# A gated attention mixer's silu, written as z/(1+exp(-z)): the exponential on ScalarE, the rest on VectorE

## The chip, the core and the metric
The kernel runs on one core of a Trainium2 chip. The core has five engines that run side by side: TensorE (PE, matmuls; PEld is its weight load), VectorE (DVE), ScalarE (ACT), GpSimd (POOL) and SyncE (SP), which here issues the DMAs. They are held in order by semaphores only. The metric is the device time of one execution in microseconds (us), lower is better.

## The reference
Two blocks of two layers each, on 256 tokens of width 1024, in float32. The first block (attention, short convolution, state-space scan, feed-forward) is not touched. The second block has two mixers; the first (`mixer_a`, three dilated window attentions) is not touched either. The change is in `mixer_b`, the second mixer: a sliding-window attention with 16 heads and 2 key heads, whose output is multiplied by the silu of a gate z and then projected.

```python
def mixer_b(x, w_in, sinks, w_out, cos, sin):
    q, k, v, z = split_cols(x @ w_in, [B_WIDTH, B_KV, B_KV, B_WIDTH])
    q = apply_rope(q.reshape(B_, S, B_HEADS, HEAD_DIM), cos, sin).reshape(B_, S, B_KV_HEADS, G, HEAD_DIM)
    k = apply_rope(k.reshape(B_, S, B_KV_HEADS, HEAD_DIM), cos, sin)
    v = v.reshape(B_, S, B_KV_HEADS, HEAD_DIM)
    o, _ = banded_attention(q, k, v, B_WINDOW - 1, sinks)
    o = o.reshape(B_, S, B_WIDTH).astype(x.dtype)
    return (o * jax.nn.silu(z)) @ w_out
```
silu(z) is z/(1+exp(-z)). After the mixer come a layer norm, a gated projection of a second input, and the output.

## The kernel before
The host code makes one list `steps`, and every engine walks through this one list in its order and emits its own part of each step. So the order on each engine is fixed by hand. A matrix product is cut into *units* of 256 output columns. The weights of a unit are loaded by SyncE into one of three `raw` buffers and split in two halves (k 0 to 3 and 4 to 7), each into a rounded part `whi` (ScalarE copy, L1592) and a rest `wlo` (VectorE subtraction, L2157). TensorE then does three matmuls for each product (`mm3`, L1050 to L1052: hi x hi, hi x lo, lo x hi), 24 of 256 columns for each half of a unit, into one of the PSUM banks 0 to 2 in turn. Bank 5 takes the attention output, banks 3, 4, 6 and 7 the scores and transposes.

In the second mixer (`i == 1`, L812 to L821) the units are, in this order: keys and values `bkv`, queries aq0, aq1, aq2, gate az0, query aq3, gates az1, az2, az3, and then the output projection `out2` with four units. Each gate unit is two blocks of 128 gate channels by 256 tokens, in one bank (128x512 in float32). The attention goes by *pairs* of heads, p = 0 to 7, whose steps are set between the halves of the units by `b_slots` (L783):
- `att2_first`, `att2_second`: scores on TensorE (L1416); on VectorE mask and maximum (L2731), sinks and sign (L2742, L2744, L2748); on ScalarE the exponential with its sum (L2011) and that of the sink (L2016).
- `att2_turn`: VectorE adds the sink and takes the reciprocal of the sums, four numbers for each of 128 partitions (L2760, L2761); GpSimd multiplies the probabilities by it (L2926); TensorE transposes them (L1444) into banks 4 and 7; ScalarE copies them out to `APT` (L2035).
- `att2_pv`: TensorE multiplies by the values into bank 5 (L1470, L1473); VectorE multiplies this by the gate's silu `AZ` into `YA` (L2781); ScalarE rounds it to `HA` (L2041), VectorE takes the rest `LA` later (L2179). `out2` reads HA and LA.

A pair's pv may not start before VectorE has read the one before out of bank 5 (`acquire(5, (s_ya, ip))`, L1455). The gate unit az`hq` serves pairs 2hq and 2hq + 1: az0 is needed first by pair 0, az1 by pair 2, az2 by pair 4, az3 by pair 6. ScalarE takes the silu of a gate unit from its bank to `AZ[hq % 2]` as soon as its turn in the list comes (L1746 to L1749), and signals `s_z2`; both the bank and the product at L2781 are released by that signal. VectorE has nothing to do for a gate unit but the weight splits that stand ahead of every unit (`unit`, L2223), and the deferred pieces in `late`. `chain` (L2168) on VectorE makes the next instruction wait for the one just issued.

In the slots around the gate units, in this order: az0, then pv of pair 0 and the scores of pair 4; half of aq3, pv of pair 1; ...; az1, pv 2, scores of pair 7; half of az2, pv 3; az2, pv 4; half of az3, pv 5; az3, pv 6; first half of the first out2 unit, pv 7.

Of the kernel before, what the change touches and what calls it, by code (L numbers as in the profile page):

```python
# [17 lines left out]
ALU = mybir.AluOpType  # L18
# [151 lines left out]
def build(nc, A, out, counts):  # L170
# [151 lines left out]
    s_ya = signal("ya")  # L322
    s_yh = signal("yh")
    s_z2 = signal("z2")


    base = (nc.sbuf_base + 63) // 64 * 64
# [576 lines left out]
    def both(b):  # L904

        return b.rearrange("p (b t) -> p b t", b=2)
# [669 lines left out]
    def _(engine):  # L1576
# [52 lines left out]
        def unit(u):  # L1629
# [67 lines left out]
            elif kind == "ff1":  # L1697
                l, g, i = u.key
                t = t_of(l)
                sl = slice(t[0], t[1])  # L1700
                for bi in (0, 1):
                    j = 2 * i + bi
                    b = bank(u, bi)
                    if j >= 2:
                        act.wait_ge(s_fq, s_fq.at((l, g, j - 2)))
                    elif g > 0:
                        act.wait_ge(s_fq, s_fq.at((l, g - 1, 6 + j)))
                    f(R32[j % 2][:, sl], b[:, 0:t[1] - t[0]], ACT.Relu).then_inc(*s_relu.tick(u.key + (bi,)))
                for bi in (0, 1):
                    j = 2 * i + bi  # L1710
                    act.wait_ge(s_relu, s_relu.at(u.key + (bi,)))
                    f(hi_part("f", l, None, j, sl), R32[j % 2][:, sl], ACT.Square).then_inc(*s_fh.tick((l, g, j)))
            elif kind == "ff2":
                l, g, i = u.key
                if g == 3:
                    for m in (2 * i, 2 * i + 1):
                        late.append(lambda l=l, m=m: square_y(l, "ffn", m))
                    for m in (2 * i, 2 * i + 1) if i < 3 else ():
                        late.append(lambda l=l, m=m: gate_y(l, "ffn", m))
            elif kind in ("aq", "ak") or kind == "bkv":  # L1720
                n = 2 if kind != "bkv" else 1
                b = both(bank(u, n - 1))
                key = u.key + ((kind,) if kind != "bkv" else ("kb",))
                if sh_turn[0] >= 2:
                    act.wait_ge(s_rope2, s_rope2.at(("n", sh_turn[0] - 2)))
                for q in range(4):
                    o = q ^ 1
                    ins = f(SH[sh_turn[0] % 2][32 * q:32 * q + 32, 0:n, :], b[32 * o:32 * o + 32, 0:n, :], ACT.Copy)  # L1728
                ins.then_inc(*s_sh2.tick(key))
                sh_turn[0] += 1  # L1730
                if kind == "bkv":
                    for tt in (0, 1):
                        b = bank(u, 1)
                        b = banks[bank_of[(u.id, 1 + tt)]]

                        src = b[:, 0:P].rearrange("p (h d) -> p h d", h=2)
                        for dup in (0, 1):
                            ins = f(AV[0][:, 0:2, tt, 64 * dup:64 * dup + 64], src, ACT.Copy)
                        ins.then_inc(*s_vb2.tick(tt))
            elif kind == "av":  # L1740
                i, hq, g = u.key
                if hq >= 2:
                    act.wait_ge(s_o2, s_o2.at((i, 2 * (hq - 2) + 1)))
                f(AV[hq % 2][:, g, :, :], both(bank(u, 1)), ACT.Copy).then_inc(*s_v2.tick(u.key + (0,), u.key + (1,)))
            elif kind == "az":
                i, hq, g = u.key  # L1746
                if hq >= 2:
                    act.wait_ge(s_ya, s_ya.at((i, 2 * (hq - 2) + 1)))
                f(AZ[hq % 2], both(bank(u, 1)), ACT.Silu).then_inc(*s_z2.tick(u.key + (0,), u.key + (1,)))  # L1749
            elif kind == "proj":  # L1750
                i, part = u.key
                for n in range(2):
                    if n == 1:
                        splits(u.halves_next)
                    m = 2 * part + n
                    f(PJ[:, 2 * m:2 * m + 2, :], both(bank(u, n)), ACT.Copy).then_inc(*s_pj.tick((i, m)))
                splits(u.halves_ahead)
            elif kind == "gate":
                i, j = u.key
                if j >= 2:  # L1760
                    act.wait_ge(s_gmul, s_gmul.at((i, j - 2)))
                f(SH[j % 2], both(bank(u, 1)), ACT.Sigmoid).then_inc(*s_sg.tick(u.key))
                if i == 0:
                    def part():
                        act.wait_ge(s_x2_new, s_x2_new.at((0, 2 * j + 1)))
                        f(parts2("x2", 1)[0][:, 2 * j:2 * j + 2, :], XT[:, 2 * j:2 * j + 2, SEQ:T], ACT.Copy)\
                            .then_inc(*s_x2_hi.tick((1, 2 * j), (1, 2 * j + 1)))

                    late.append(part)
# [374 lines left out]
    def _(engine):  # L2144
# [78 lines left out]
        def unit(u):  # L2223
# [70 lines left out]
            elif kind == "ff2":  # L2294
                l, g, i = u.key
                t = t_of(l)
                sl = slice(t[0], t[1])
                for bi in (0, 1):
                    m = 2 * i + bi
                    if u.packed:  # L2300
                        y, b, keys = YM[:, 2 * i:2 * i + 2, sl], both(bank(u, 1)), (u.key + (0,), u.key + (1,))
                    else:
                        y, b, keys = YM[:, m, sl], bank(u, bi)[:, 0:t[1] - t[0]], (u.key + (bi,),)
                    if bi == 0 or not u.packed:
                        if g == 0:
                            ins = v.tensor_copy(y, b)
                        else:
                            dve.wait_ge(s_f_add, s_f_add.at((l, g - 1, i, bi)))
                            ins = v.tensor_tensor(y, y, b, ALU.add)
                        ins.then_inc(*s_f_add.tick(*keys))  # L2310
                    if g == 3 and m < KC - 2:
                        late.append(lambda m=m: add_square(("p", l, "ffn"), m, sl))
            elif kind in ("aq", "ak", "bkv"):
                if kind != "aq" or u.key[0] == 0:
                    rope_unit(u)
            elif kind == "out2":
                i, j = u.key
                v.scalar_tensor_tensor(out=V32[:, 2 * j:2 * j + 2, :], in0=XT[:, 2 * j:2 * j + 2, SEQ:T], scalar=ALPHA, in1=both(bank(u, 1)),
                                       op0=ALU.mult, op1=ALU.add).then_inc(*s_v32.tick(u.key + (0,), u.key + (1,)))
                for bi in (0, 1):  # L2320
                    m = 2 * j + bi

                    def add(i=i, m=m):
                        dve.wait_ge(s_v32, s_v32.at((i, m // 2, m % 2)))
                        total = RR[0][:, 0, :]
                        if m == 0:
                            ins = v.tensor_copy(total, V32[:, 0, :])
                        else:
                            dve.wait_ge(s_ln_acc, s_ln_acc.at((i, "mean", m - 1)))
                            ins = v.tensor_tensor(total, total, V32[:, m, :], ALU.add)  # L2330
                        ins.then_inc(*s_ln_acc.tick((i, "mean", m), *([(i, "mean")] if m == KC - 1 else [])))

                    late.append(add)
            elif kind == "proj":
                splits(u.halves_ahead)
            elif kind == "gate":
                i, j = u.key
                m = slice(2 * j, 2 * j + 2)
                dve.wait_ge(s_sg, s_sg.at(u.key))
                dve.wait_ge(s_pj, s_pj.at((i, j)))  # L2340
                dve.wait_ge(s_ln_x, s_ln_x.at((i, 2 * j + 1)))
                v.tensor_tensor(RR[j % 2], SH[j % 2], PJ[:, m, :], ALU.mult).then_inc(*s_gmul.tick((i, j)))
                dve.wait_ge(s_gmul, s_gmul.at((i, j)))
                v.tensor_tensor(XT[:, m, SEQ:T], XT[:, m, SEQ:T], RR[j % 2], ALU.add).then_inc(*s_x2_new.tick((i, 2 * j), (i, 2 * j + 1)))
                if i == 0:
                    def part():
                        dve.wait_ge(s_x2_hi, s_x2_hi.at((1, 2 * j + 1)))
                        dve.wait_ge(s_x2_new, s_x2_new.at((0, 2 * j + 1)))
                        hi, lo = parts2("x2", 1)
                        rest(lo[:, m, :], XT[:, m, SEQ:T], hi[:, m, :], s_parts2.tick((1, 2 * j), (1, 2 * j + 1)))  # L2350

                    late.append(part)
# [619 lines left out]
```

## Time and profile before
| | |
|---|---|
| median of 3 runs | 1640.62 us (1637.44 to 1644.46) |
| profiled execution, its own time | 1640.4 us |
| its span | 1638.4 us |
| TensorE busy | 1518.7 us (93%) |
| VectorE busy | 971.9 us (59%) |
| ScalarE busy | 914.6 us (56%) |
| GpSimd busy | 34.2 us (2%) |
| mean granted TensorE clock | 0.969 |

The profile is one execution; all times in the rows are microseconds from the start of its span unless they are marked ns. The second mixer's work lies from about 1476 us (its first queries and keys) to about 1569 us (where TensorE goes on with its output projection). A granted clock of 1.00 is 2.4 GHz, 0.50 is 1.2 GHz. ACT_TABLE_LOAD on ScalarE loads the tables of another set of functions.

### The profile page before, as it was taken

The numbers are of one execution on the slowest core, as the hardware profiler recorded it, in microseconds if no ns is written. First come the engines' busy times: TensorE is split into PE (matmuls) and PEld (weight loads), VectorE is DVE, ScalarE is ACT, GpSimd is POOL, SyncE is SP. The second block draws the span as 40 slices with busy tenths as digits, with TensorE's granted clock in tenths as the row PEclk, the third lists the DMA queues.
The fourth block names the chain that finished last, engine by engine and source line by source line (L and its number), as shares of the span: only waits on it lengthen the run. The fifth ranks groups of instructions, "written<-read, shape, count | busy, mean of one in ns | idle before, by whom it ended". The sixth has DMA issues, their size and how long they took to land.

```text
span 1638.4 us, 25449 instructions
## 1 busy us (share of the span) xinstructions
PE 1518.7 (93%) x10131; PEld 1273.4 (78%) x10131; DVE 971.9 (59%) x1565; ACT 914.6 (56%) x1510; POOL 34.2 (2%) x74
## 2 busy tenths in 40 slices
PE   5999998989999999979988899998999999889887
PEld 3687455758888888838855799998999999888787
DVE  2464567473343434474767766667676767577555
ACT  5654666462232423464665655566786868377745
POOL 3000000000000000000000000000000000001200
PEclk9999899989999999999998999998999999999999
DMA  7731445342433233343316576653634434343332
GB/s 248 236 102 52 155 151 184 121 136 79 153 103 100 81 103 103 111 129 88 118 38 198 181 228 189 197 196 120 232 130 155 155 131 153 104 155 106 101 103 78
DMA packets 223638, 225.37 MB, mean 138 GB/s; under 512 B 8234, under 2 KB 222064, under 8 KB 223472
## 3 DMA queue, kind: packets, MB, share of 16 engines
q1 hardware_dynamic: 222816, 223.63, 42.3%
q8 instruction: 80, 1.31, 0.3%
q14 instruction: 38, 0.31, 0.1%
q0 software_dynamic: 704, 0.12, 0.0%
HBM read 222.68 MB, written 1.05 MB: 137 GB/s over the span
## 4 chain that ended last, share of the span: by engine, by line
PE 72%; DVE 13%; ACT 10%; issue 2%; DMA 1%; POOL 1%; DVEq 0%; ACTq 0%; POOLq 0%
PE bank L1050 21%; PE bank L1052 20%; PE bank L1051 20%; DVE wlo L2157 2%; PE bank L1098 2%; ACT whi L1592 2%; ACT SH L1728 1%; PE bank L1256 1%; PE bank L1416 1%; PE bank L1444 1%; PE bank L1371 1%; ACT AP L2011 1%; POOL vrow L2904 1%; DVE AP L2731 1%; DMA raw<-in_w_out_dram 1%
## 5 line engine op out<-in xcount | busy, mean ns | idle before, releaser
L2157 DVE TENSOR_TENSOR wlo<-raw,whi 128x1024 fp32r<-128x1024 f32 (+2 forms) x322 | 387.9, 1208 | 258.5 <-ACT whi L1592 253.5
L1592 ACT ACTIVATE whi<-raw 128x1024 fp32r<-128x1024 f32 (+2 forms) x322 | 336.0, 1046 | 272.8 <-PE bank L1052 250.0
L1050 PE MATMUL bank<-HH,whi 128*128 128x512 f32 (+2 forms) x640 | 245.9, 384 | 19.9 <-DVE HL L2179 16.9
L1051 PE MATMUL bank<-HL,whi 128*128 128x512 f32 (+2 forms) x640 | 242.2, 378 | 0.0
L1052 PE MATMUL bank<-HH,wlo 128*128 128x512 f32 (+2 forms) x640 | 241.8, 378 | 0.0
L1050 PE MATMUL bank<-HA,whi 128*128 128x256 f32 x576 | 165.2, 287 | 13.8 <-DVE LA L2179 5.2
L1051 PE MATMUL bank<-LA,whi 128*128 128x256 f32 x576 | 162.1, 281 | 0.0
L1052 PE MATMUL bank<-HA,wlo 128*128 128x256 f32 x576 | 161.9, 281 | 0.0
L1050 PEld LDWEIGHTS bank<-HH,whi 128*128 128x128 f32 (+1 forms) x640 | 121.1, 189 | 49.3 <-issue 17.8
L1052 PEld LDWEIGHTS bank<-HH,wlo 128*128 128x128 f32 (+1 forms) x640 | 121.3, 190 | 23.6 <-issue 0.5
L1051 PEld LDWEIGHTS bank<-HL,whi 128*128 128x128 f32 (+1 forms) x640 | 121.3, 190 | 22.5 <-issue 0.9
L1050 PEld LDWEIGHTS bank<-HA,whi 128*128 128x128 f32 x576 | 111.0, 193 | 17.8 <-issue 11.6
L1051 PEld LDWEIGHTS bank<-LA,whi 128*128 128x128 f32 x576 | 111.1, 193 | 0.0
L1052 PEld LDWEIGHTS bank<-HA,wlo 128*128 128x128 f32 x576 | 110.9, 192 | 0.0
L1050 PE MATMUL bank<-FH,whi 128*128 128x512 f32 x256 | 100.3, 392 | 0.0
L1051 PE MATMUL bank<-FL,whi 128*128 128x512 f32 x256 | 99.7, 389 | 0.0
L1052 PE MATMUL bank<-FH,wlo 128*128 128x512 f32 x256 | 99.6, 389 | 0.0
L1050 PE MATMUL bank<-HX,whi 128*128 128x256 f32 x320 | 90.8, 284 | 4.3 <-DVE HXL L2179 4.3
L1051 PE MATMUL bank<-HXL,whi 128*128 128x256 f32 x320 | 89.9, 281 | 0.0
L1052 PE MATMUL bank<-HX,wlo 128*128 128x256 f32 x320 | 89.9, 281 | 0.0
L1050 PE MATMUL bank<-YH,whi 128*128 128x256 f32 x264 | 78.0, 296 | 5.1 <-DVE YL L2883 4.5
L1728 ACT ACTIVATE SH<-bank 32x512 f32<-32x512 f32 (+1 forms) x116 | 67.5, 582 | 16.9 <-PE bank L1052 15.4
(377 smaller groups left out, 3077.2 us busy)
## 6 DMA issues: line engine op xcount, KB each, us to landing
raw<-in_w_ff_dram SPq DMA_DIRECT2D x64, 1024.0 KB, 5.4
raw<-in_w_mod_dram SPq DMA_DIRECT2D x48, 1024.0 KB, 5.2
raw<-in_a_w_in_dram SPq DMA_DIRECT2D x40, 1024.0 KB, 5.1
raw<-in_w_in_dram SPq DMA_DIRECT2D x18, 1024.0 KB, 5.3
raw<-in_b_w_in_dram SPq DMA_DIRECT2D x9, 1024.0 KB, 5.3
raw<-in_w_out_dram SPq DMA_DIRECT2D x8, 1024.0 KB, 5.4
raw<-in_ple_w_gate_dram SPq DMA_DIRECT2D x8, 1024.0 KB, 5.3
raw<-in_a_w_out_dram SPq DMA_DIRECT2D x4, 1024.0 KB, 5.1
```

What stands on the lines that cost most here:

```text
L1050: nc.tensor.matmul(o, wh, xh, start=start, stop=False, skip_group_check=shared)
L1051: nc.tensor.matmul(o, wh, xl, start=False, stop=False, skip_group_check=shared)
L1052: return nc.tensor.matmul(o, wl, xh, start=False, stop=stop, skip_group_check=shared)
L1098: ins = nc.tensor.matmul(b[32 * q:32 * q + 32, 0:256], cs[:, k, :], raw[u.id % RAW_SLOTS][:, k * 256:k * 256 + 256], start=turn == 0, stop ...
L1256: nc.tensor.matmul(b[:, 0:nk], QT[0:QK, h, q0:q0 + P], KT[0:QK, h, 0:nk], start=True, stop=True)\
L1371: nc.tensor.matmul(b[:, 0:t[1] - t[0]], ones, SQ[k % 2][:, t[0]:t[1]], start=k == 0, stop=k == KC - 1)\
L1416: ins = nc.tensor.matmul(dst[e][:, g * n:(g + 1) * n], q_, k_[:, 0:n], start=True, stop=True)
L1444: ins = nc.tensor.transpose(b[:, to:to + P], att_p(ip, e)[:, src:src + P], ident)
L1592: f(whi[h % HALF_SLOTS][:, 0:n], raw[u.id % RAW_SLOTS][:, (h % 2) * n:(h % 2) * n + n], ACT.Copy)\
L1728: ins = f(SH[sh_turn[0] % 2][32 * q:32 * q + 32, 0:n, :], b[32 * o:32 * o + 32, 0:n, :], ACT.Copy)
L2011: f(p_[:, a:a + n], p_[:, a:a + n], ACT.Exp, bias=small[:, neg:neg + 1], scale=SCALE, accum_out=small[:, total:total + 1]).then_inc(*s_e2. ...
L2157: v.tensor_tensor(wlo[h % HALF_SLOTS][:, 0:n], raw[u.id % RAW_SLOTS][:, (h % 2) * n:(h % 2) * n + n], whi[h % HALF_SLOTS][:, 0:n].bitcast( ...
```

## The change
For the units az0 to az3 of the second mixer ScalarE writes exp(-z) instead of silu(z) to `AZ`, and signals a new semaphore `s_ez2`. VectorE, when the unit's turn comes in its own list (behind the unit's splits and the deferred pieces), adds 1, takes the reciprocal, and multiplies by z read from the bank, all in place in `AZ`, each instruction waiting for the one before. The last of them gives the signal `s_z2` that ScalarE gave before; so the bank is held until then too. The first mixer keeps its silu. Nothing else is moved.

```diff
@@ -322,6 +322,7 @@
+    s_ez2 = signal("ez2")
@@ -1746,7 +1747,10 @@
                 i, hq, g = u.key
                 if hq >= 2:
                     act.wait_ge(s_ya, s_ya.at((i, 2 * (hq - 2) + 1)))
-                f(AZ[hq % 2], both(bank(u, 1)), ACT.Silu).then_inc(*s_z2.tick(u.key + (0,), u.key + (1,)))
+                if i == 0:
+                    f(AZ[hq % 2], both(bank(u, 1)), ACT.Silu).then_inc(*s_z2.tick(u.key + (0,), u.key + (1,)))
+                else:
+                    f(AZ[hq % 2], both(bank(u, 1)), ACT.Exp, scale=-1.0).then_inc(*s_ez2.tick(u.key))
@@ -2313,6 +2317,12 @@
             elif kind in ("aq", "ak", "bkv"):
                 if kind != "aq" or u.key[0] == 0:
                     rope_unit(u)
+            elif kind == "az" and u.key[0] == 1:
+                z = AZ[u.key[1] % 2]
+                dve.wait_ge(s_ez2, s_ez2.at(u.key))
+                chain(v.tensor_scalar(z, z, 1.0, None, ALU.add))
+                chain(v.reciprocal(z, z))
+                v.tensor_tensor(z, both(bank(u, 1)), z, ALU.mult).then_inc(*s_z2.tick(u.key + (0,), u.key + (1,)))
             elif kind == "out2":
```

## Rows read from the trace of the kernel before
**Rows 1.** The page, part 4: shares of the chain that ended last.
```profile
PE 72%; DVE 13%; ACT 10%; issue 2%; DMA 1%; POOL 1%; DVEq 0%; ACTq 0%; POOLq 0%
```
**Rows 2.** Windows: length, busy PE, PEld, DVE, ACT, POOL; clock; DMA share, GB/s.
```profile
1520.00:1530.00 10.00, 7.03 (x50) 6.86 (x50) 5.24 (x18) 8.12 (x25) 1.90 (x4) 0.83 0.02 4
```
**Rows 3.** Groups by line, ScalarE: its table loads; count, busy us, mean ns, idle before.
```profile
L1749 ACT ACT_TABLE_LOAD x7 | 9.0, 1283 | 1.7 <-PE bank L1052 1.7
L2011 ACT ACT_TABLE_LOAD x7 | 9.0, 1283 | 9.2 <-DVE small L2744 6.5 <-DVE small L2736 2.6
```
**Rows 4.** Timeline of ScalarE, second mixer: start us, length us, what, idle before.
```profile
1514.39 1.28 ACT L1749 ACT_TABLE_LOAD   x1
...
1518.87 1.28 ACT L2011 ACT_TABLE_LOAD   x1 [1.52 <-DVE small L2744]
...
1539.71 1.28 ACT L1749 ACT_TABLE_LOAD   x1 [0.27 <-PE bank L1052]
1541.01 0.60 ACT L1749 ACTIVATE AZ<-bank 128x512 f32<-128x512 f32 x1
...
1545.23 1.28 ACT L2011 ACT_TABLE_LOAD   x1 [1.66 <-DVE small L2744]
...
1551.14 1.28 ACT L1749 ACT_TABLE_LOAD   x1
...
1558.66 0.60 ACT L1749 ACTIVATE AZ<-bank 128x512 f32<-128x512 f32 x1 [0.26 <-PE bank L1052]
```
**Rows 5.** Timeline of VectorE, second mixer, around the four gate units.
```profile
1515.00 0.18 DVE L2761 RECIPROCAL small<-small 128x4 f32<-128x4 f32 x1
1516.41 0.42 DVE L2781 TENSOR_TENSOR YA<-bank,AZ 128x256 f32<-128x256 f32 x1 [1.23 <-ACT AZ L1749]
...
1540.08 0.18 DVE L2761 RECIPROCAL small<-small 128x4 f32<-128x4 f32 x1
1541.74 0.42 DVE L2781 TENSOR_TENSOR YA<-bank,AZ 128x256 f32<-128x256 f32 x1 [1.48 <-ACT AZ L1749]
...
1552.63 0.43 DVE L2179 TENSOR_TENSOR LA<-YA,HA 128x256 fp32r<-128x256 f32 x1
1553.17 0.42 DVE L2781 TENSOR_TENSOR YA<-bank,AZ 128x256 f32<-128x256 f32 x1
...
1558.06 2.36 DVE L2157 TENSOR_TENSOR wlo<-raw,whi 128x1024 fp32r<-128x1024 f32 x2
1560.45 0.42 DVE L2781 TENSOR_TENSOR YA<-bank,AZ 128x256 f32<-128x256 f32 x1
```
**Rows 6.** Timeline of TensorE: pv of pairs 1, 5, 7, transposes of pair 3, restart.
```profile
1516.89 0.65 PE L1470 MATMUL bank<-APT,AV 128*64 128x256 f32 x4 [0.90 <-DVE YA L2781]
...
1525.42 1.51 PE L1444 MATMUL bank<-ident_sb,AB 128*128 128x128 f32 x6 [2.97 <-ACT APT L2035]
...
1553.65 0.65 PE L1470 MATMUL bank<-APT,AV 128*64 128x256 f32 x4 [0.45 <-DVE YA L2781]
...
1562.32 0.65 PE L1470 MATMUL bank<-APT,AV 128*64 128x256 f32 x4
...
1568.90 0.43 PE L1050 MATMUL bank<-HA,whi 128*128 128x256 f32 x1 [2.76 <-DVE wlo L2157]
```
**Rows 7.** Groups of VectorE by form: count, busy us, mean ns, idle before.
```profile
L2205 DVE TENSOR_TENSOR RR<-bank,rope_sb 128x512 f32<-128x512 f32 x28 | 19.4, 691 | 30.7 <-ACT SH L1728 27.0 <-PE bank L1052 3.5
...
L2358 DVE TENSOR_SCALAR CV<-XP,VT 128x512 f32<-128x512 f32 x12 | 5.8, 486 | 7.7 <-ACT XP L1672 7.5
...
L2761 DVE RECIPROCAL small<-small 128x4 f32<-128x4 f32 x8 | 1.4, 178 | 0.3
...
L2557 DVE RECIPROCAL RD<-DN 128x64 f32<-128x64 f32 x2 | 1.1, 552 | 0.1
```
**Rows 8.** Timeline of GpSimd: its products for pair 7.
```profile
1552.74 2.07 POOL L2926 TENSOR_TENSOR AP<-AP,small 128x128 f32<-128x128 f32 x4 [10.44 <-DVE small L2761]
```
**Rows 9.** Line L2742 alone: ns min/median/max of its 16 instructions.
```profile
L2742 DVE TENSOR_SCALAR small<-small,sinks_sb x16: 215/225/682, 1491.6 to 1544.7; 128x2 f32<-128x2 f32 x16
```

## The prediction
> **What bounds the kernel now.** I read four things. First the page's chain of the work that ended last: TensorE holds 72% of it, VectorE 13%, ScalarE 10% [rows 1]. This share is an average over a kernel of some 1,640 us, and the change touches only the second mixer, so the next question is what the chain looks like there. The chain listed in order of time goes, between 1484 and 1569 us, mostly through ScalarE and VectorE: a score's maximum on VectorE, an exponential on ScalarE, a silu, a product on VectorE, a weight split. The windows say the same in numbers: TensorE is busy for 7.03 of the 10 us from 1520 [rows 2], where its transposes waited 2.97 us for ScalarE's copy APT [rows 6]. There TensorE waits for the other two; a microsecond put on VectorE between them is felt.
>
> Then the two engines' timelines. ScalarE runs 7 table loads before silus (L1749) and 7 before attention exponentials (L2011) in the whole kernel [rows 3]. Of these, the second mixer has the five listed at 1514.39, 1518.87, 1539.71, 1545.23 and 1551.14 [rows 4], and one more before its first exponential, which stays. On VectorE one sees who stands behind the silu: the products YA<-bank,AZ at 1516.41, 1541.74, 1553.17 and 1560.45 (pairs 0, 2, 4 and 6, the first users of each gate unit) [rows 5]. The first two start 0.12 to 0.13 us after the silu's end (1541.01 + 0.60 = 1541.61, product at 1541.74) [rows 4, 5]. And behind the product stands TensorE: bank 5 holds the attention output of one pair, and the next pair's pv matmul may not start before the product has read it. pv of pair 1 had waited 0.90 us for the product, pv of pair 5 0.45 us [rows 6].
>
> **What is removed.** Four silus become four exponentials of the same shape; I count them at the same 0.60 us [rows 4]. Exp is already the function at L2011 and Copy ran after it without a load, so behind that first load no switch is left in the mixer: five loads go, 5 x 1.283 = 6.4 us of ScalarE. From start of load to start of silu is 1541.01 - 1539.71 = 1.30 us, and I use 1.3 for each that lies on the path. The Trainium skill, page "ScalarE: Activation LUTs", section "What ACT_TABLE_LOAD costs", adds a drain of about 1380 ns to every switch, 2.66 us together. By it each of the path's loads would give back 1.36 us more. The rows show no such drain: the load at 1539.71 is followed by the silu 0.02 us after its end. What the rule would give is a rival below.
>
> **What is added.** Per gate unit, on VectorE, one after the other: an addition, a reciprocal and a product, each on 128x512 numbers, each waiting for the one before.
> - The addition: TENSOR_SCALAR 128x512 takes 486 ns [rows 7].
> - The product with one operand in PSUM: TENSOR_TENSOR 128x512 RR<-bank takes 691 ns [rows 7].
> - The reciprocal of 128x512: the trace has none. The largest is 128x64 with 552 ns, the next 128x4 with 178 ns [rows 7]. The slope is (552 - 178) / 60 = 6.23 ns for each number of a partition, so 178 + 508 x 6.23 = 3.34 us. Taken in proportion it would be 8 x 552 = 4.42 us. The lower end is the rate of the other operations, some 0.69 us. I take 3.34, because the 128x64 row is already far above the cost of an ordinary operation and a fixed start-up plus a slope fits both rows.
> The page "VectorE: DVE Perf Modes" of the Trainium skill, section "First, the fixed hardware budget", says that the reciprocal is an iterative divide with a repeat count of 8. With 8 times the (0.69 - 0.42) / 256 = 1.05 ns that a product takes per number [rows 5, 7] that is, as an estimate, 8.4 ns and 4.5 us, and the sum would be that of the first rival; the rows here say about 6 times, not 8, and I stay with the rows. It is the rule that speaks most against this change.
> With two gaps of 0.03 us (L2760 to L2761 is such a pair) the added piece is 0.49 + 3.34 + 0.69 + 0.06 = 4.58 us, 18.3 us of VectorE in all, for 6.4 us of ScalarE. The two are not on the path alike, so I walk the path, with "+" for the delay against the trace of before.
>
> **Unit 0.** Exp may start at 1514.39 and ends at 1514.99, but VectorE is free only after its reciprocal of pair 3 (1515.00 + 0.18) [rows 5]. So 1515.21 + 4.58 = 1519.79, and the product of pair 0 starts at 1519.82 instead of 1516.41: +3.4. Queued behind it on VectorE: pair 4's maximum, then pair 1's product. TensorE's pv of pair 1 goes from 1516.89 to 1520.3. Pair 4's exponential loses its table load: 3.4 - 1.3 = +2.1, and ScalarE's splits, copies and the exponentials of pairs 5 and 6 follow it in order, all +2.1. TensorE's own lateness is absorbed: its next transposes (1525.42) waited 2.97 us for ScalarE [rows 6] and get only ScalarE's +2.1.
>
> **Unit 1.** Exp starts at 1539.71 + 2.1 = 1541.81 without a load, ends at 1542.41; VectorE is free at 1540.08 + 0.18 + 2.1 = 1542.36, so it is just the Exp that counts. Plus 0.13, 4.58 and 0.03: pair 2's product at 1547.15 instead of 1541.74, +5.4. Pair 7's maximum stands behind it, and pair 7's exponential loses its load: 5.4 - 1.3 = +4.1.
>
> **Unit 2.** ScalarE's Exp is early (its load gone as well), so this saving is worth nothing: VectorE arrives at the unit only with the end of LA at 1552.63 + 0.43 + 4.1 = 1557.16. Here GpSimd works in parallel on pair 7, from 1552.74 + 4.1 = 1556.84 for 2.07 us [rows 8]. A TENSOR_SCALAR beside GpSimd's products was held up: L2742 took 682 ns at most beside them, 215 at least [rows 9]. So the addition gets 0.46 us more. 1557.19 + 0.46 + 4.58 = 1562.23, product of pair 4 at 1562.26 instead of 1553.17: +9.1. TensorE's pv of pair 5, before at 1553.65, stands idle in front of it for about 6 us.
>
> **Unit 3.** Its Exp waits for TensorE to end the unit: 1558.66 + 9.1 = 1567.8 at full clock. After the idle piece before 1525.42 the clock was at half speed for about a third of a 10 us window (granted clock 0.83 from 1520 to 1530 [rows 2], that is 1.2 instead of 2.4 GHz for 3.4 us, 1.7 us lost), and this stall is longer; so +1.7, Exp from 1569.5 to 1570.1. VectorE's splits end at 1558.06 + 2.36 + 9.1 = 1569.5. The piece runs from 1570.2 to 1574.8, product of pair 6 at 1574.8 instead of 1560.45: +14.3. Without the half clock it would be VectorE that counts, and +13.7.
>
> **The end.** pv of pair 7 started at 1562.32 although its bank was free at 1560.45 + 0.42 = 1560.87: 1.45 us of slack, 1.3 after a signal's 0.13. So 14.3 - 1.3 = +13.0 for it. From there to TensorE's restart at 1568.90 [rows 6] all is a chain: product of pair 7, its copy, two splits. Nothing behind 1569 knows the change, so +13.0 carries to the end. The profiled execution's own time is 1640.4 us (span 1638.4), and the median of the runs is 1640.62, the same. 1640.4 + 13.0 = 1653.4.
>
> **The rivals.**
> - The reciprocal costs 4.42 us instead of 3.34. For it: the proportion with the 128x64 row. Against: the 128x4 row shows a small fixed part only. Four units in series: 4 x 1.08 = +4.3, so 1657.7.
> - The large reciprocal runs as fast as other operations, 0.69 us (not slower). For it: no row of a large one exists. Against: 128x64 took 552 ns. The place is the four pieces; each is then 1.93 us. The same walk gives +0.8, -0.5, +0.1, -1.2, +1.2, +3.1 and at the end +1.8: 1642.2. It decides from about 2.2 us of reciprocal downward, since every microsecond of it counts some four times and +8.2 is the bound below.
> - A switch holds ScalarE longer than its load. The most that a row allows is the idle 1.52 us ahead of the load at 1518.87 [rows 4], if that were a drain and not, as listed, a wait for the maximum. On the path lie three switches (pairs 4 and 7, unit 1): 3 x 1.5 = 4.5 more given back, +8.5; with some of unit 0's, about 1648. Against it: the maximum really ends just there, and nothing lies between load and silu. This is the page's drain as named above; its figure would give nearly the same.
> - The change doesn't do what it says: Exp at L1749 and Exp at L2011 would still be separated by loads. Then 3 x 1.3 + 1.1 come back: 1658.4. Against: it is the same function.
> - GpSimd holds the addition for its whole stretch, in units 1 and 2: 1.9 + 1.3 = +3.2, so 1656.6. I keep it within the forecast's range.
>
> **How the numbers follow.** The forecast 0.69, the dearer reciprocal 0.13, not separated by function 0.03; these are slower. The cheap reciprocal 0.12 and the longer switch 0.02 lie within 0.5%. 0.5% is 8.2 us, about what a measurement of this kernel can tell from no change (the runs of before spread by 7 us). Faster by that would need more than all five loads give (6.4 us), so 0.01. Slower 0.85, same 0.14, faster 0.01. Range: low 1648, for a reciprocal near 2.2 us; without half clock and GpSimd's lock it would be 1652.4. High 1660: the dearer reciprocal and most of GpSimd's term.
>
> **What would show it.** ScalarE: table loads at the gate line only 4 instead of 7, at L2011 5 instead of 7. VectorE: four reciprocals 128x512, 3.3 us each, starting right behind the addition. TensorE: a wait of some 6 us for the product before pv of pair 5, of 4 us before that of pair 1, and a half clock behind the first of them. The second mixer (from 1476 to the restart near 1569) is 13 us longer and nothing before or after differs. I am wrong if the reciprocal is off by a factor, since the sum is nearly four times its length, or if TensorE's waits for YA products do not grow.

## The result and the profile after
The changed kernel takes 1656.7 us (median of 7 runs, 1648.35 to 1659.81); the kernel before takes 1643.33 us in the same 7 rounds (1637.44 to 1645.64). The ratio is 1.0083 with a 95% interval of 1.0066 to 1.0100, so by the ratio the change costs 13.6 us, between 11 and 16 (the medians differ by 13.4). The forecast was +13.0 us and 1653.4 us. It started from 1640.4 us, and the kernel before has since measured 1643.33 us, so 2.9 of the 3.3 us between 1653.4 and 1656.7 are the starting point's.

The page of the changed kernel, parts 1 and 4. The first lines are busy us, share of the span and count of each engine; the last is the chain that ended last.

```profile
span 1657.5 us, 25464 instructions
## 1 busy us (share of the span) xinstructions
PE 1529.9 (92%) x10131; PEld 1284.8 (78%) x10131; DVE 989.6 (60%) x1577; ACT 908.1 (55%) x1505; POOL 34.7 (2%) x74
...
PE 71%; DVE 15%; ACT 10%; issue 2%; DMA 1%; POOL 1%; DVEq 0%; ACTq 0%; POOLq 0%
```
VectorE is busy 989.6 - 971.9 = 17.7 us longer, ScalarE 914.6 - 908.1 = 6.5 us shorter, and VectorE has two points more of the chain [rows 1]. But nothing here says that the one falls on the path and the other only in part. For that the groups and the timelines are needed. The groups by line that answer to [rows 3] and the new ones of [rows 7] (count, busy us, mean ns, idle before):

```profile
L2015 ACT ACT_TABLE_LOAD x5 | 6.4, 1283 | 6.0 <-DVE small L2754 3.3 <-DVE small L2746 2.6
L1751 ACT ACT_TABLE_LOAD x4 | 5.1, 1283 | 1.6 <-PE bank L1053 1.6
...
L2324 DVE RECIPROCAL AZ<-AZ 128x512 f32<-128x512 f32 x4 | 13.4, 3353 | 0.1
L2325 DVE TENSOR_TENSOR AZ<-bank,AZ 128x512 f32<-128x512 f32 x4 | 2.8, 692 | 0.1
L2323 DVE TENSOR_SCALAR AZ<-AZ 128x512 f32<-128x512 f32 x4 | 1.8, 446 | 0.8 <-ACT AZ L1753 0.7
```
Table loads before exponentials 5 instead of 7, before the gates 4 (all in the first mixer) instead of 7, as forecast. The reciprocal takes 3353 ns, where 3.34 us were worked out from its 128x64 and 128x4 rows.

VectorE around units 0 and 2, the timeline that answers to [rows 5]:

```profile
1519.87 0.18 DVE L2771 RECIPROCAL small<-small 128x4 f32<-128x4 f32 x1
1520.08 0.43 DVE L2323 TENSOR_SCALAR AZ<-AZ 128x512 f32<-128x512 f32 x1
1520.55 3.35 DVE L2324 RECIPROCAL AZ<-AZ 128x512 f32<-128x512 f32 x1
1523.93 0.69 DVE L2325 TENSOR_TENSOR AZ<-bank,AZ 128x512 f32<-128x512 f32 x1
1524.66 0.42 DVE L2791 TENSOR_TENSOR YA<-bank,AZ 128x256 f32<-128x256 f32 x1
...
1552.24 0.42 DVE L2791 TENSOR_TENSOR YA<-bank,AZ 128x256 f32<-128x256 f32 x1
...
1562.31 0.51 DVE L2323 TENSOR_SCALAR AZ<-AZ 128x512 f32<-128x512 f32 x1
1562.85 3.35 DVE L2324 RECIPROCAL AZ<-AZ 128x512 f32<-128x512 f32 x1
1566.24 0.69 DVE L2325 TENSOR_TENSOR AZ<-bank,AZ 128x512 f32<-128x512 f32 x1
1566.96 0.42 DVE L2791 TENSOR_TENSOR YA<-bank,AZ 128x256 f32<-128x256 f32 x1
...
1579.45 0.42 DVE L2791 TENSOR_TENSOR YA<-bank,AZ 128x256 f32<-128x256 f32 x1
```
And TensorE, which answers to [rows 6]: the first scores, pv of pairs 1, 3, 5 and 7, the transposes of pair 3 and the restart.

```profile
1493.98 0.93 PE L1417 MATMUL bank<-AK,AQ 64*128 64x128 f32 x8 [2.04 <-DVE AQ L2217]
...
1525.13 1.12 PE L1471 MATMUL bank<-APT,AV 128*64 128x256 f32 x4 [4.27 <-DVE YA L2791]
...
1533.31 0.82 PE L1445 MATMUL bank<-ident_sb,AB 128*128 128x128 f32 x6
...
1552.72 0.65 PE L1471 MATMUL bank<-APT,AV 128*64 128x256 f32 x4 [0.71 <-DVE YA L2791]
...
1567.44 1.12 PE L1471 MATMUL bank<-APT,AV 128*64 128x256 f32 x4 [6.48 <-DVE YA L2791]
...
1579.93 0.65 PE L1471 MATMUL bank<-APT,AV 128*64 128x256 f32 x4 [2.11 <-DVE YA L2791]
...
1586.50 0.58 PE L1051 MATMUL bank<-HA,whi 128*128 128x256 f32 x1 [2.68 <-DVE wlo L2161]
```
Before pv of pairs 1 and 5, where TensorE had waited 0.90 and 0.45 us for the product [rows 6], it now waits 4.27 and 6.48 us; before pv of pairs 3 and 7, where it had not waited, 0.71 and 2.11 us. The four matmuls behind the two long waits take 1.12 instead of 0.65 us: the clock has fallen. The wait of the transposes for ScalarE (2.97 us [rows 6]) is gone in return. The windows show TensorE's short busy time and the granted clock of 0.72 and 0.77 (columns as in [rows 2]):

```profile
1520.00:1530.00 10.00, 5.73 (x31) 3.84 (x30) 8.12 (x21) 3.22 (x11) 2.22 (x5) 0.72 0.30 100
1560.00:1570.00 10.00, 3.52 (x22) 2.61 (x21) 8.00 (x11) 3.40 (x7) 2.25 (x4) 0.77 0.33 105
```

The two profiled spans differ by 1657.5 - 1638.4 = 19.1 us, more than the medians. To see what belongs to the change I measure a **stretch**: from the first scores of the second mixer on TensorE to the restart behind pair 7. Before, the scores start at 1489.12 (the same row of the kernel before is shown with the repeat below) and the restart is at 1568.90 [rows 6], 79.78 us. After, 1586.50 - 1493.98 = 92.52 us. So 12.7 us lie in the stretch, 4.9 us ahead of it, where no line was changed, and 1.5 us behind it. The experiments are read by this stretch. It is steadier than a whole run, but not exact: a second profile of the kernel before gives 81.0 instead of 79.8 us, one of the changed kernel 92.5 again (last experiment). So the change costs 11.5 to 12.7 us in the stretch, and a difference of about 1 us between two profiles can be the execution's.

Most of that uncertainty has one place: the piece from the scores of pair 6 to pv of pair 2 on TensorE, the same 32 matmuls in every kernel. It took 5.34 us in the first profile of before, at a granted clock of 0.68, and 6.57 us in the second, at 0.54; time times clock is 3.6 and 3.5, so the clock accounts for the difference. It is called **the clock's place** below.

### The profile page after: what moved, and what is told of

It is laid out like the page before. It is cut to its first block, busy times and chain, and to the rows that moved or that the text cites. A ratio compares the mean times of both kernels' runs of the same rounds, so it can differ in the third digit from the quotient of the medians.

```text
span 1657.5 us, 25464 instructions
## 1 busy us (share of the span) xinstructions
PE 1529.9 (92%) x10131; PEld 1284.8 (78%) x10131; DVE 989.6 (60%) x1577; ACT 908.1 (55%) x1505; POOL 34.7 (2%) x74
## 3 DMA queue, kind: packets, MB, share of 16 engines
q8 instruction: 80, 1.31, 0.3%
## 4 chain that ended last, share of the span: by engine, by line
PE 71%; DVE 15%; ACT 10%; issue 2%; DMA 1%; POOL 1%; DVEq 0%; ACTq 0%; POOLq 0%
PE bank L1051 20%; PE bank L1053 20%; PE bank L1052 20%; DVE wlo L2161 2%; ACT SH L1729 2%; PE bank L1099 2%; ACT whi L1593 2%; PE bank L1257 1%; DVE AP L2741 1%; PE bank L1445 1%; PE bank L1417 1%; DVE AZ L2324 1%; PE bank L1372 1%; ACT AP L2015 1%; DMA raw<-in_w_out_dram 1%
## 5 line engine op out<-in xcount | busy, mean ns | idle before, releaser
L1051 PE MATMUL bank<-HA,whi 128*128 128x256 f32 x576 | 166.0, 288 | 13.5 <-DVE LA L2183 5.2
L1729 ACT ACTIVATE SH<-bank 32x512 f32<-32x512 f32 (+1 forms) x116 | 67.5, 582 | 15.0 <-PE bank L1053 13.5
```

The source lines that it names most:

```text
L1051: nc.tensor.matmul(o, wh, xh, start=start, stop=False, skip_group_check=shared)
```

## The experiments
**Is it the length of the reciprocal?** The changed kernel with a cheap operation in the reciprocal's place, and with two reciprocals.

```diff
-                chain(v.reciprocal(z, z))
+                chain(v.tensor_tensor(z, z, z, ALU.mult))
```


> The reciprocal is replaced by a product z*z of the same 128x512 (0.69 us instead of 3.35), so the gate's values are wrong; addition, waits and last product stay. I measure the stretch from the first scores of the second mixer on TensorE (1489.12 before, 1493.98 after) to TensorE's restart behind pair 7 (1568.90, 1586.50): 79.8 us before, 92.5 after. Theory (the length of the four VectorE pieces is in series): the walk of the prediction gives +1.8 against before, 81.6 us, and in all about 11 us less than with the change. Rival (it is the hand-over between the engines, the chained waits and the half clock, not the length): 88 us or more.

Measured: the stretch is 1572.65 - 1489.13 = 83.5 us; median 1644.96 us over 10 runs, ratio to before 1.0018 (0.9992 to 1.0045). So 9.0 us of the 12.7 go away with the length of four instructions (the products in their place took 0.80 us each, so 4 x 2.55 = 10.2 us were taken out), and the rest is not told from no change in whole runs. The rival (88 or more) falls. The stretch is 1.9 us more than the 81.6 expected. TensorE's timeline of this kernel shows where most of it comes from:

```profile
1533.74 1.65 PE L1417 MATMUL bank<-AK,AQ 64*128 64x128 f32 x8 [0.85 <-DVE AQ L2217]
...
1540.41 0.65 PE L1471 MATMUL bank<-APT,AV 128*64 128x256 f32 x4
...
1556.26 0.65 PE L1471 MATMUL bank<-APT,AV 128*64 128x256 f32 x4 [2.22 <-DVE YA L2791]
1557.38 1.51 PE L1445 MATMUL bank<-ident_sb,AP 128*128 128x128 f32 x6 [0.25 <-ACT APT L2039]
```
The clock's place took 1540.41 - 1533.74 = 6.67 us, 1.3 more than in the first profile of before, at a granted clock of 0.54. Up to the exponential of pair 4 the walk holds to 0.1 us (30.57 us behind the first scores, 0.5 before the kernel before, as walked); at the product of pair 2 the kernel is already 1.6 us above it. The transposes of pair 5 run at half clock too (1.51 instead of 0.87 us for six), but at the product of pair 6 the kernel is still 1.6 us above the walk.

```diff
                 chain(v.reciprocal(z, z))
+                chain(v.reciprocal(z, z))
```


> The reciprocal is done twice in a row, so the gate's values are wrong. Theory (all four pieces in series): 4 x 3.39 = 13.5 us more than with the change, the stretch 106 us, and one or two more from the clock. Rival (only the units that TensorE was seen to wait for most, 0 and 2, count): 6.8 us more, 99 us.

Measured: the stretch is 107.65 us, 15.1 more than with the change; median 1666.33 us over 4 runs, ratio 1.0152 (1.0099 to 1.0205). The added reciprocals are 3353 ns each, 13.5 us with their gaps. Counted from the first scores, the products of pairs 0, 2, 4 and 6 come 3.4, 7.0, 10.5 and 14.5 us later than with the change, so each of the four units adds 3.4 to 4.0 us: all four are in series, and the rival (99) falls. The last 0.7 us come behind pv of pair 7, whose matmuls run at half clock (1.12 instead of 0.65 us). TensorE's waits before pv of pairs 1, 3, 5 and 7:

```profile
1523.42 1.12 PE L1471 MATMUL bank<-APT,AV 128*64 128x256 f32 x4 [7.57 <-DVE YA L2792]
...
1554.66 1.12 PE L1471 MATMUL bank<-APT,AV 128*64 128x256 f32 x4 [5.11 <-DVE YA L2792]
...
1572.77 1.12 PE L1471 MATMUL bank<-APT,AV 128*64 128x256 f32 x4 [8.13 <-DVE YA L2792]
...
1589.27 1.12 PE L1471 MATMUL bank<-APT,AV 128*64 128x256 f32 x4 [5.50 <-DVE YA L2792]
```
They have grown by 3.3, 4.4, 1.7 and 3.4 us. A wait grows only by what TensorE is not late itself: at pair 5 it arrives 8.8 us later than with the change (1572.77 - 8.13 - 1488.87 against 1567.44 - 6.48 - 1493.98), and the product 10.5 us later.

**What are the table loads worth?** Once without VectorE's part, once with the loads put back.

```diff
-                    f(AZ[hq % 2], both(bank(u, 1)), ACT.Exp, scale=-1.0).then_inc(*s_ez2.tick(u.key))
+                    f(AZ[hq % 2], both(bank(u, 1)), ACT.Exp, scale=-1.0).then_inc(*s_z2.tick(u.key + (0,), u.key + (1,)))
...
-            elif kind == "az" and u.key[0] == 1:
-                z = AZ[u.key[1] % 2]
...
```


> ScalarE's Exp stays and gives the signal itself; VectorE does nothing for the gates, so the gate is exp(-z) and the values are wrong. It shows what the five table loads are worth alone. Theory (walk): pair 4's exponential 2.5 us earlier, then TensorE becomes the one that is late and takes another 0.8: the stretch 76.5 us, 3.3 less than before. Rival 1 (all five loads lie on the path): 6.4 less, 73.4. Rival 2 (a switch costs twice its load): 7 less or more, 73 or under.

Measured: the stretch is 1568.26 - 1490.72 = 77.5 us, 2.2 less than before; median 1639.23 us, ratio 0.9983 (0.9958 to 1.0007). Against the second profile of before it is 3.4 us less. So six microseconds of ScalarE, the whole reward of the change, are worth 2 to 3.5 on the path even when they cost nothing. The walk had 3.3. This profile took 0.6 us more than the others in its first scores (1.52 instead of 0.93 us for the eight matmuls) and 0.65 us more in the clock's place (5.99 us at 0.60), together a little more than the 1.0 us by which it lies above 76.5. Both rivals, 73 and 73.4, are excluded. TensorE is what is last now: it is busy for 10.00 of the 10 us from 1540 and again from 1550, where it had 10.00 and 9.20 before.

```diff
-                    f(AZ[hq % 2], both(bank(u, 1)), ACT.Exp, scale=-1.0).then_inc(*s_ez2.tick(u.key))
+                    f(AZ[hq % 2], both(bank(u, 1)), ACT.Silu).then_inc(*s_ez2.tick(u.key))
```


> The changed kernel, but ScalarE does Silu instead of Exp, so all table loads are back and VectorE's pieces stay; the gate's values are wrong. Theory: three loads and most of a fourth lie on the path, 3 x 1.3 + 1.1 = 5.0 us more than with the change, the stretch 97.5. Rival (the loads hide behind VectorE's longer pieces): 92.5 to 94.

Measured: 1585.13 - 1487.01 = 98.1 us, 5.6 more than with the change (5.0 expected). ScalarE has 7 loads again at L2015. By steps, against the change: pair 0's product 1.3 us later, pair 4's exponential 2.6, pair 7's exponential 6.2. That is about four loads of 1.3 us and 1.2 us of the clock's place (6.60 us at 0.54 against 5.37 at 0.68 with the change); some 0.6 us are won back before unit 3. So beside VectorE's long pieces four of the five loads lie on the path in full, 4.4 to 5.6 us, against 2 to 3.5 us for all five where no piece stands there and TensorE is last. What a load is worth hangs on which engine is last at that point.

**Does one unit behave as walked?** Only unit 3 with VectorE's piece, the others as before.

```diff
-                if i == 0:
+                if i == 0 or hq < 3:
...
-                    f(AZ[hq % 2], both(bank(u, 1)), ACT.Exp, scale=-1.0).then_inc(*s_ez2.tick(u.key))
+                    f(AZ[hq % 2], both(bank(u, 1)), ACT.Silu).then_inc(*s_ez2.tick(u.key))
...
-            elif kind == "az" and u.key[0] == 1:
+            elif kind == "az" and u.key[:2] == (1, 3):
```


> Units 0 to 2 as before the change (Silu, signalled by ScalarE). Unit 3: Silu on ScalarE and then VectorE's whole piece (addition, reciprocal, product), so its values are wrong; no table load differs from before. Theory: pair 6's product 4.5 us later, 1.3 of it is slack before pair 7's pv: the stretch 79.8 + 3.2 = 83.0 us. Rival (pv of pair 7 has no slack or more than a wait's worth): 84.3, or 80 if TensorE's first half of the output projection covers it.

Measured: 1578.04 - 1493.42 = 84.6 us, beyond both numbers. Taken apart, pv of pairs 6 and 7 (TensorE's timeline of this kernel):

```profile
1564.46 0.65 PE L1471 MATMUL bank<-APT,AV 128*64 128x256 f32 x4
...
1571.47 0.65 PE L1471 MATMUL bank<-APT,AV 128*64 128x256 f32 x4 [3.12 <-DVE YA L2791]
```
From pair 6 to pair 7 it is 7.01 us here and was 1562.32 - 1558.50 = 3.82 us before (pv of pair 6 started at 1558.50 there): +3.2, as expected. The other 1.7 us lie before unit 3, where this kernel does what the kernel before does: 1.3 us in the clock's place (1545.53 - 1538.89 = 6.64 us, at 0.54) and 0.4 us ahead of it, where the first scores took 1.31 instead of 0.93 us. So they are no effect of the edit; the second profile of before has the same 1.2 us at the same place. How a delay at unit 0 alone travels is not measured: with only unit 0's piece on VectorE the kernel deadlocks.

**Which part of the work stands in front?** The same arithmetic in blocks of 256 columns, the second one set ahead of the odd pair's wait.

```diff
+        def gate(u, blk):
+
+            gates[u.key[1]] = u
+            z, ps = AZ[u.key[1] % 2][:, blk, :], both(bank(u, 1))[:, blk, :]
+            dve.wait_ge(s_ez2, s_ez2.at(u.key))
+            chain(v.tensor_scalar(z, z, 1.0, None, ALU.add))
+            chain(v.reciprocal(z, z))
+            v.tensor_tensor(z, ps, z, ALU.mult).then_inc(*s_z2.tick(u.key + (blk,)))
...
             elif kind == "az" and u.key[0] == 1:
...
+                gate(u, 0)
...
             buf, blk = (p // 2) % 2, p % 2
+            if i == 1 and blk == 1:
+                gate(gates[p // 2], 1)
             dve.wait_ge(s_o2, s_o2.at(ip))
```


> The same arithmetic as the change, but for each gate unit VectorE does at first only the block of 256 columns that the even pair needs, and the other block ahead of its wait for the odd pair's pv. The VectorE work grows slightly (two short pieces instead of one long). Theory (only what stands before a product and a pv counts): a short piece is 0.3 + 1.77 + 0.42 = 2.5 us; the walk gives 0 at pair 4's exponential, 0 at pair 7's, +2.5 at pair 4's product, +5 at pair 6's and pair 7's, so the stretch from the first scores to the restart is 85 us, 7.5 less than with the change (92.5). Rival (VectorE's total time is what counts): 92.5 or more.

Measured: 1573.88 - 1486.94 = 86.9 us, 5.6 less than with the change (7.5 expected), median 1645.93 us, ratio to before 1.0035 (1.0013 to 1.0056), against 1.0083. VectorE's groups show that its work has grown, not shrunk (8 reciprocals, 14.0 us instead of 13.4):

```profile
L2235 DVE RECIPROCAL AZ<-AZ 128x256 f32<-128x256 f32 x8 | 14.0, 1754 | 0.3
```
So it is the position of the work, not its sum, that costs. The rival falls. Of the 1.9 us that were missed, 1.1 are there at pair 4's product (+3.6 us against before, +2.5 walked). Another 0.8 come up to pair 6's product (+6.9, +5 walked), where the transposes of pair 5 run at half clock (1.36 instead of 0.87 us). The first part is not explained. What ends last is no longer a pv: pair 7's pv comes 5.5 us later than before, its product 7.2, because VectorE's second block stands between.

**A form without reciprocal.** silu(z) = 0.5 z (1 + tanh(z/2)).

```diff
-                    f(AZ[hq % 2], both(bank(u, 1)), ACT.Exp, scale=-1.0).then_inc(*s_ez2.tick(u.key))
+                    f(AZ[hq % 2], both(bank(u, 1)), ACT.Tanh, scale=0.5).then_inc(*s_ez2.tick(u.key))
...
-                chain(v.tensor_scalar(z, z, 1.0, None, ALU.add))
-                chain(v.reciprocal(z, z))
-                v.tensor_tensor(z, both(bank(u, 1)), z, ALU.mult).then_inc(*s_z2.tick(u.key + (0,), u.key + (1,)))
+                v.scalar_tensor_tensor(out=z, in0=z, scalar=1.0, in1=both(bank(u, 1)), op0=ALU.add, op1=ALU.mult).then_inc(*s_z2.tick(u.key + (0,), u.key + (1,)))
...
+                v.scalar_tensor_tensor(out=YA[buf][:, blk, :], in0=banks[5][:, 0:SEQ], scalar=0.5, in1=AZ[buf][:, blk, :], op0=ALU.mult, op1=ALU.mult).then_inc(*s_ya.tick(ip))
```


> silu(z) = 0.5 z (1 + tanh(z/2)): ScalarE takes Tanh, VectorE one SCALAR_TENSOR_TENSOR (t + 1) * z of 0.69 us, and the 0.5 goes into the product L2791 (0.48 instead of 0.42 us). No reciprocal. If Tanh needs no load beside Exp, theory: nearly what the kernel with Exp alone gives (77.5 us), 78 us, some 1.7 us less than before the change and 14.5 less than with it; TensorE's waits before pv of pairs 1 and 5 under 0.5 us. Rival (Tanh is loaded apart from Exp): all loads back, the stretch 81 to 83.

Measured: 1566.79 - 1488.65 = 78.1 us, as expected, 14.4 less than with the change. Median 1637.08 us over 12 runs, ratio to before 0.9983 (0.9959 to 1.0007): clearly ahead of the changed kernel, and against the kernel before not told from no change. Tanh needs no load beside Exp: L2015 has 5 loads, the gates 4 (all in the first mixer), as with the change. ScalarE and VectorE at unit 0 of this kernel:

```profile
1513.96 0.60 ACT L1753 ACTIVATE AZ<-bank 128x512 f32<-128x512 f32 x1
...
1514.77 0.69 DVE L2323 SCALAR_TENSOR_TENSOR AZ<-AZ,bank 128x512 f32<-128x512 f32 x1
1515.48 0.42 DVE L2792 SCALAR_TENSOR_TENSOR YA<-bank,AZ 128x256 f32<-128x256 f32 x1
```

The same in the first mixer too, where TensorE has little idle time:

```diff
-                if i == 0:
-                    f(AZ[hq % 2], both(bank(u, 1)), ACT.Silu).then_inc(*s_z2.tick(u.key + (0,), u.key + (1,)))
-                else:
-                    f(AZ[hq % 2], both(bank(u, 1)), ACT.Tanh, scale=0.5).then_inc(*s_ez2.tick(u.key))
+                f(AZ[hq % 2], both(bank(u, 1)), ACT.Tanh, scale=0.5).then_inc(*s_ez2.tick(u.key))
...
-            elif kind == "az" and u.key[0] == 1:
+            elif kind == "az":
...
```


> The Tanh form of e_tanh in the first mixer as well: eight more table loads (4 before gates, 4 before exponentials) may go there, 10.3 us of ScalarE, for 4 x 0.7 us of VectorE. Theory (what counts is the engine that the stage waits for): in the first mixer TensorE is busy 271.3 of the 280 us from 1160 on, so ScalarE's gain there is worth 0 to 2 us, and the kernel comes out like e_tanh, within 0.3% of before, at 1635 to 1639 against 1638. Rival (every load is worth its length, as some were in the second mixer): 10 us less than before the change.

Measured: median 1636.68 us over 12 runs, ratio 0.9980 (0.9959 to 1.0001), the stretch of the second mixer 77.9 us. The page gives ScalarE 898.9 us, 9.2 less than with the change, and nothing of that is seen in the time. The rival's 10 us would be a ratio of 0.994, below the interval, and falls. Removing table loads where TensorE is the bound gives nothing that these runs can tell from nothing (the interval is 7 us wide).

**What belongs to the execution?** Both kernels once more.

> The kernel before once more. In the profile of before, 120 us from 960 on hold 1062 matmuls, in that of the changed kernel 1021, long before the code that the change touches, both at a granted clock of 1.00. Theory (the pace is of the execution, not of the program): here 1061 or 1021, either may come, and the arrival at the second mixer's first scores lies between 1487 and 1494. Rival (the pace is set by the program): 1061 or 1062 again.

> The changed kernel once more. The stretch from the first scores to the restart again 92.5 us, 1.7 more or less by where the half clock falls (79.8 before the change). Theory of the pace as for the kernel before: 1061 or 1021 matmuls from 960 to 1080. Rival (program): 1021 again.

Measured: before again, the stretch 1574.11 - 1493.12 = 81.0 us, and from 960 to 1080 us it now holds 1021 matmuls; after again, 1579.12 - 1486.62 = 92.5 us, and 1061 matmuls. Here are the first scores in the first profile of before, and then the window of 120 us in that profile and in the repeat (columns as in [rows 2]; the counts in brackets are instructions):

```profile
1489.12 0.93 PE L1416 MATMUL bank<-AK,AQ 64*128 64x128 f32 x8 [2.04 <-DVE AQ L2213]
```

```profile
960.00:1080.00 120.00, 120.00 (x1062) 120.00 (x1061) 76.34 (x77) 59.36 (x66) 0.00 (x0) 1.00 0.61 195
```

```profile
960.00:1080.00 120.00, 120.00 (x1021) 120.00 (x1020) 73.22 (x74) 56.38 (x62) 0.00 (x0) 1.00 0.58 187
```
So the two programs have changed places: the pace of that stage is of the execution. The rival falls. The changed kernel's first profile happened to be one with 1021, and 41 matmuls fewer in 120 us are 4.6 us. The six profiles with 1061 or 1062 reach the first scores at 1486.62 to 1489.12, the six with 1021 at 1489.13 to 1493.98. So the 4.9 us ahead of the mixer go with the pace; that nothing else is in them was not shown.

The repeats also show how steady the stretch is: 92.5 twice, and 79.8 and 81.0. The 1.2 us between the two of before lie in one piece, between the scores of pair 6 and pv of pair 2. TensorE in the first profile, then in the repeat:

```profile
1534.22 0.98 PE L1416 MATMUL bank<-AK,AQ 64*128 64x128 f32 x8 [0.85 <-DVE AQ L2213]
...
1539.56 0.65 PE L1470 MATMUL bank<-APT,AV 128*64 128x256 f32 x4
```

```profile
1538.21 1.65 PE L1416 MATMUL bank<-AK,AQ 64*128 64x128 f32 x8 [0.85 <-DVE AQ L2213]
...
1544.78 0.65 PE L1470 MATMUL bank<-APT,AV 128*64 128x256 f32 x4
```
5.34 and 6.57 us for the same matmuls of the same program, at a granted clock of 0.68 and 0.54; 5.34 x 0.68 is 3.6 and 6.57 x 0.54 is 3.5, so the clock accounts for the difference.

## Why the prediction was right
Point by point, with the delay in the profile counted from the first scores (subtract 1489.12 before, 1493.98 after):

| step | forecast | measured |
|---|---|---|
| reciprocal 128x512 | 3.34 us | 3.35 us |
| product of pair 0 | +3.4 | +3.4 |
| exponential of pair 4 (1520.17 before, 1527.13 after) | +2.1 | +2.1 |
| product of pair 2 | +5.4 | +5.6 |
| product of pair 4 | +9.1 | +8.9 |
| product of pair 6 | +14.3 | +14.1 |
| pv of pair 7, restart | +13.0 | +12.7 |
| whole runs, by the ratio | +13.0 | +13.6 (11 to 16) |

The mechanism held step by step. That the end is met to 0.3 us is in part luck: against the second profile of before the restart comes 11.5 us later.

- **The reciprocal's length** was the term that decided. The straight line through the 128x4 and 128x64 rows held over a factor of eight: 178, 552, 1754 (128x256, in the split kernel) and 3353 ns, 6.25 ns a number. The proportion (4.42 us), and with it the estimate of 4.5 us from the repeat count of 8 that the Trainium skill states on its page "VectorE: DVE Perf Modes", section "First, the fixed hardware budget", are refuted as a duration; a sixfold cost per number is what the rows give. The rival with a fast reciprocal fell with the same number, and the cheap kernel shows that it would have been within 0.5% (ratio 1.0018, 0.9992 to 1.0045).
- **Four in series.** Shown by both doses: 10.2 us less of VectorE in the four pieces gives back 9.0 us, with the clock's place 1.3 us longer than with the change, and 13.5 us more cost 15.1. In the second, each of the four units moved the next product by 3.4 to 4.0 us.
- **The loads.** By the prediction three on the path and most of a fourth: 5.0 us; putting them back cost 5.6, of which some 1 us may be the clock's. The drain that the Trainium skill, on its page "ScalarE: Activation LUTs", section "What ACT_TABLE_LOAD costs", adds to a switch isn't borne out: three and a bit switches of 2.66 us would have been over 8 us.
- **Half clock before unit 3.** From pv of pair 5 to unit 3's Exp it took 6.73 us (1574.17 - 1567.44) and 5.01 before (1558.66 - 1553.65): the 1.7 us of the prediction. Exp was expected at 1569.5 and came at 1574.17 - 4.86 = 1569.3. The splits of VectorE ended as Exp began, so the addition waited 0.67 us for it, as stated.
- **Two readings of the walk were off and cost little.** "Just the Exp that counts" at unit 1: Exp ended at 1547.46 and VectorE's own reciprocal of pair 6 at 1547.63, with the addition right behind at 1547.67, so VectorE was last, and pair 2's product came +5.6 instead of +5.4. "TensorE's own lateness is absorbed" at unit 0: the transposes of pair 3 came 3.0 us later and not 2.1, with their wait of 2.97 us used up; the next exponential still came +2.1.
- **GpSimd.** This small term was wrong: the addition that ran beside GpSimd's products for its whole length (unit 2) took 0.51 us against 0.43 at the other units, not 0.46 us more. GpSimd became slower in turn: its four products took 2.25 us at unit 2 where they had taken 2.07 [rows 8]. The addition itself was 0.43, not 0.49 us. These two errors are part of why pair 4's product came +8.9 and not +9.1.
- **"Nothing behind 1569 knows the change"**: from the restart to the end it is 1657.5 - 1586.5 = 71.0 us after and 69.5 before; the repeats have 1644.4 - 1574.1 = 70.3 (before) and 1647.9 - 1579.1 = 68.8 (after). So the 1.5 us are of the execution.

What stays open: 1.1 us of the split kernel's 1.9 above its walk, and 0.6 us of the cheap kernel's 1.9, of which 1.3 are the clock's place. The kernels of the experiments have one profile each, so differences of 1 us between stretches say nothing by themselves. Why the clock is at half speed for more of the same matmuls in one execution than in another is not shown.

## What to carry to other kernels
A trade of one engine's time for another's is priced by who is last at that point, not by the sums: here 6.4 us of ScalarE were worth 2 to 3.5 alone and 4.4 to 5.6 next to longer VectorE pieces, while 18 us of VectorE cost what stood ahead of the product that freed a bank. A reciprocal over a full tile is a large instruction on VectorE (3.35 us for 128x512, five times a product); look for a form without one, such as the Tanh form, which needed no table load beside Exp. Compare two profiles by a stretch around the change that begins and ends with the same instructions, since whole runs of one program differ by more than such a change (the kernel before ran from 1631.81 to 1653.37 us), and take two profiles of each: the stretch itself moved by 1.2 us.

## What the runs showed of the hardware that was not expected
Matmuls back to back at a granted clock of 1.00 run at one of two paces in the feed-forward stage: 120 us hold 1061 or 1062 matmuls in some executions and 1021 in others (0.1133 and 0.1177 us from start to start at 256 columns), with the same program, and the same in each 40 us of the 120 (356 and 342 in the two profiles of before). Of the twelve profiled executions six had the one and six the other. The DMA share is lower with the slower pace (0.58 to 0.60 against 0.60 to 0.61), but which is cause was not tried.

The clock's place took between 4.6 and 6.7 us over the twelve profiles. In four of them, among them the repeat of the kernel before, it took 6.6 to 6.7 us, each at a granted clock of 0.54; the first profile of the same program had 5.3 us at 0.68.
